# A two-block transformer in float32 on one core: five reorderings on TensorE around short waits

## What is computed

```python
def first_block(x, c, ...):
    h = _rmsnorm(x, norm_g[l]) * (1.0 + scale[:, None, :]) + shift[:, None, :]
    proj = h @ w_in[l]
    (q_a, k_a, v_a, z_a, q_b, k_b, v_b, z_b, f_logit, g_logit) = jnp.split(proj, split_points, axis=-1)
    y_a = _from_heads(_stick_breaking(q_a, k_a, v_a))
    y_a = (y_a * jax.nn.silu(z_a)) @ w_o_sb[l]
    log_f = jax.nn.log_sigmoid(f_logit + b_forget[l])
    cum_log_f = jnp.cumsum(log_f, axis=1).transpose(0, 2, 1)
    y_b = _from_heads(_forgetting_attention(q_b, k_b, v_b, cum_log_f))
    ...
    x = x + gate[:, None, :] * (merged @ w_out[l])
    return _rmsnorm(x, final_g)

def second_block(x, mem, ...):
    h = h + hybrid_mixer(rmsnorm(h, norm_mix_g[l]), ...)
    h = h + cross_attention(rmsnorm(h, norm_cross_g[l]), rmsnorm(mem, norm_mem_g[l]), ...)
    h = h + conv_ffn(rmsnorm(h, norm_ffn_g[l]), ...)
    return rmsnorm(h, norm_final_g[l])
```

## Time and profile before

| | us |
|---|---|
| median of 3 runs | 1424.27 (1421.89 to 1424.64) |
| the profiled execution's own time | 1422.05 |
| its span in the trace | 1420.2 |
| TensorE busy with matmuls | 1303.5 (92%), 6164 records |
| VectorE / GpSimd / ScalarE busy | 794.9 / 751.6 / 575.3 |
| mean granted TensorE clock | 0.969 of full |

### The profile page before, as it was taken

How to read it: one execution, slowest core, us unless ns; L and a number is a source line. 1 busy time by engine, 2 the same in 40 slices (tenths; PEclk the granted TensorE clock), 3 DMA queues, 4 the chain that set the end, 5 groups by cost and what they waited for, 6 DMA issues and landing times.

```text
span 1420.2 us, 16997 instructions
## 1 busy us (share of the span) xinstructions
PE 1303.5 (92%) x6164; PEld 1062.7 (75%) x6164; DVE 794.9 (56%) x1339; ACT 575.3 (41%) x926; POOL 751.6 (53%) x866
## 2 busy tenths in 40 slices
PE   3689999988999899899998789999999999999996
PEld 2567878867888777687776688787778888888874
DVE  5746767513333346687688554775537724651644
ACT  3354556425555335422335454443434322331331
POOL 4353443332333375476443377832647966885771
PEclk9999999999999999999999799999999999999998
DMA  8531222322333552222222334321222332323221
GB/s 303 178 104 44 68 67 101 115 68 80 99 108 114 194 157 85 82 86 93 75 61 67 112 106 145 119 75 45 90 90 63 108 111 90 104 92 102 89 75 59
DMA packets 41699, 142.80 MB, mean 101 GB/s; under 512 B 4624, under 2 KB 5008, under 8 KB 40464
## 3 DMA queue, kind: packets, MB, share of 16 engines
q1 hardware_dynamic: 41616, 141.71, 30.8%
HBM read 131.21 MB, written 8.39 MB: 98 GB/s over the span
## 4 chain that ended last, share of the span: by engine, by line
PE 78%; DVE 12%; ACT 5%; issue 2%; DMA 1%; POOL 1%; SPq 0%; DVEq 0%; ACTq 0%; POOLq 0%
PE ps L135 77%; DVE tm L145 3%; DVE ma L148 1%; ACT wh L142 1%; ACT tm L142 1%; PE ps L139 1%; ACT L142 1%; DVE tm L148 1%; DMA con_raw<-con 1%; DVE ac L148 1%; ACT hh L142 1%; DVE sql L145 0%; DVE x L148 0%; POOL ycl L145 0%; POOL wl L145 0%
## 5 line engine op out<-in xcount | busy, mean ns | idle before, releaser
L145 POOL TENSOR_TENSOR wl<-raw,wh 128x256 fp32r<-128x256 f32 x804 | 681.5, 879 | 595.2 <-ACT wh L142 595.2
L142 ACT ACTIVATE wh<-raw 128x1024 fp32r<-128x1024 f32 x201 | 212.6, 1058 | 486.5 <-PE ps L135 474.5
L135 PE MATMUL ps<-hh,wh 128*128 128x512 f32 x872 | 345.5, 396 | 2.8 <-DVE cb L145 1.6
L135 PE MATMUL ps<-hl,wh 128*128 128x512 f32 x872 | 341.0, 391 | 0.0
L135 PE MATMUL ps<-hh,wl 128*128 128x512 f32 x872 | 340.9, 391 | 0.0
L135 PEld LDWEIGHTS ps<-hh,wh 128*128 128x128 f32 x872 | 164.9, 189 | 39.1 <-DVE cb L145 2.4
L135 PEld LDWEIGHTS ps<-hh,wl 128*128 128x128 f32 x872 | 164.3, 188 | 34.9
L135 PEld LDWEIGHTS ps<-hl,wh 128*128 128x128 f32 x872 | 164.8, 189 | 33.5 <-issue 0.5
L148 DVE SCALAR_TENSOR_TENSOR tm<-cb,par_sb,tm 128x512 f32<-128x512 f32 x88 | 87.5, 994 | 50.8 <-ACT tm L142 47.4
L145 DVE TENSOR_TENSOR tm<-tm,tm 128x512 f32<-128x512 f32 (+3 forms) x106 | 91.1, 863 | 35.3 <-ACT tm L142 32.5
L142 ACT ACTIVATE tm<-tm 128x512 f32<-128x512 f32 (+3 forms) x109 | 54.5, 532 | 86.8 <-DVE tm L148 81.2
(11 more groups left out here) (316 smaller groups left out, 2405.4 us busy)
## 6 DMA issues: line engine op xcount, KB each, us to landing
raw<-units SPq DMA_DIRECT2D x217, 512.0 KB, 3.5
kept<-ge SPq DMA_DIRECT2D x16, 256.0 KB, 2.0
tm<-kept SPq DMA_DIRECT2D x16, 256.0 KB, 3.8
tm<-gate_w SPq DMA_DIRECT2D x12, 256.0 KB, 4.1
x<-xin SPq DMA_DIRECT2D x2, 1024.0 KB, 6.6
x<-xin SPq DMA_DIRECT2D x1, 2048.0 KB, 12.2
out<-x SPq DMA_DIRECT2D x8, 256.0 KB, 2.1
kv<-kvt SPq DMA_DIRECT2D x1, 1536.0 KB, 8.5
```

What stands on the lines that cost most here:

```text
L135: return self.none if self.e is None else self.e.matmul(out, lhs, rhs, start=start, stop=stop, skip_group_check=skip)
L142: return self.none if self.e is None else self.e.activation(out, in_, func, **kw)
L145: return self.none if self.e is None else self.e.tensor_tensor(out, a, b, op)
```

## The change

Five things are done; every instruction is still there, on the same engine.

1. The first q, k, z take banks 0, 1 and 7 (`qkz_bank`), and stand in the order q, k, z in the units and on TensorE and ScalarE.
2. In head 0, the q unit of `beside_a` goes ahead of `cum_a(0)` on TensorE, and its high and low parts go ahead of `cum_a(0)` on ScalarE and VectorE.
3. `forget` is cut in three and called from `vproj("b")`: the logits' unit ahead of value unit 0, the turns ahead of unit 2, the sums ahead of unit 3.
4. In `out_proj` the unit that follows is done in three pieces: chunks 0 to 3 ahead of `add(6)`, 4 to 6 between `add(6)` and `add(7)`, 7 behind `add(7)`.
5. `spread("m2")` goes behind the next unit, u1, and on VectorE the copy of its result and `scale_x` go behind the first steps on u1 and u5.

```diff
-    u += [("aq", 0), ("az", 0), ("ak", 0)]
+    u += [("aq", 0), ("ak", 0), ("az", 0)]
...
+        def pieces(gen, name, b):
+
+            def piece(x):
+                chunks(name, b, ((0, 1, 2, 3), (4, 5, 6), (7,))[x], x == 0, x == 2, lambda k: HH[:, k, :],
+                       lambda k: HL[:, k, :], lambda k: (s_hh, gen, k), lambda k: (s_hl, gen, k))
+            return piece
...
-        def vproj(br, nm, gen):
+        def vproj(br, nm, gen, between=None):
             for u in range(4):
+                if between:
+                    between(u)
...
-        def forget():
-            hhalf("1", ("f", 0), 0, 1)
-            hhalf("1", ("f", 0), 1, 1)
-            pe.wait_ge(s_fd, "log")
+        def forget(u):
+
+            if u == 0:
+                hhalf("1", ("f", 0), 0, 1)
+                hhalf("1", ("f", 0), 1, 1)
+            if u == 2:
+                pe.wait_ge(s_fd, "log")
...
+            if u == 3:
+                pe.wait_ge(s_fd, "turned")
...
         qkz("a", 0, "q", 1)
+        qkz("a", 0, "k", 0)
+        qkz("a", 0, "k", 1)
         qkz("a", 0, "z", 0)
         qkz("a", 0, "z", 1)
-        qkz("a", 0, "k", 0)
-        qkz("a", 0, "k", 1)
...
             br, c = z_step(h)
+            if h == 0:
+                beside_a(br, c, h // 2, h % 2 == 0)
             cum_a(h)
-            beside_a(br, c, h // 2, h % 2 == 0)
+            if h:
+                beside_a(br, c, h // 2, h % 2 == 0)
...
-        forget()
-
-
-        vproj("b", "bv", "1")
+
+
+        vproj("b", "bv", "1", forget)
...
+            following(0)
             add(6)
-            following()
+            following(1)
             add(7)
+            following(2)
...
-        hhalf("m", ("u", 0), 1, 0)
         hproj("m", ("u", 4), 1)
         spread("m", 7, TM[4])
         bank[7] = (s_root, ("m", "out"))
-        spread("m2", 6, TM[3])
-        bank[6] = (s_root, ("m2", "out"))
...
             if j:
                 hproj("m", ("u", j), b0)
             bank[b0] = (s_ux, (j, 0))
+            if j == 1:
+                spread("m2", 6, TM[3])
+                bank[6] = (s_root, ("m2", "out"))
...
+    def qkz_bank(br, c, what):
+        return {"q": 0, "k": 1, "z": 7}[what] if (br, c) == ("a", 0) else {"q": 0, "k": 0, "z": 1}[what]
...
         qk_high("a", 0, "q")
         root("mem", ncol("mem", 2))
+        qk_high("a", 0, "k")
         z_gate("a", 0)
-        qk_high("a", 0, "k")
...
-        spread_out("m2", 6, YF[:, 0, :])
...
-            if j == 0:
+            if j == 1:
+                spread_out("m2", 6, YF[:, 0, :])
                 scale_x(range(KC))
```

More of the change, by code:

```diff
@@ L563, in qkz @@
         def qkz(br, c, what, part):
-            b = {"q": 0, "k": 0, "z": 1}[what]
+            b = qkz_bank(br, c, what)
             hhalf("1", (br + what, c), part, b)
@@ L638, in pv_a @@
             bank[b] = (s_gy, ("a", h))
-        def forget():
-            hhalf("1", ("f", 0), 0, 1)
-            hhalf("1", ("f", 0), 1, 1)
-            pe.wait_ge(s_fd, "log")
[L644 to L653, removed]
+        def forget(u):
[4 more added lines that the diff above has]
+                pe.wait_ge(s_fd, "log")
+                for n in range(4):
+                    last = pe.turn(PS[1][:, 8 * n:8 * n + 8], TM[1][0:8, 128 * n:128 * n + 128], con_raw[0:8, 16:24])
+                last.then_inc(*s_fp.up("turn"))
+            if u == 3:
+                pe.wait_ge(s_fd, "turned")
+                for n in range(4):
+                    for b in range(n + 1):
+                        last = pe.mm(PS[1][0:8, 128 * n:128 * n + 128], TM[0][:, 8 * b:8 * b + 8],
+                                     con_f("triu" if b == n else "one"), b == 0, b == n)
+                last.then_inc(*s_fp.up("sum"))
+                bank[1] = (s_fd, ("f",))
         vproj("a", "av", "1")
@@ L790, in out_proj @@
                 take(6)
+            following(0)
             add(6)
-            following()
+            following(1)
             add(7)
+            following(2)
             bank[7] = (s_root, (gen, "mult"))
         out_proj("wo", "m", (0, 1, 2), lambda k: mg((VBh, MG2h), k), lambda k: mg((VBl, MG2l), k),
-                 lambda k: (s_mh, k), lambda k: (s_ml, k), lambda: hhalf("m", ("u", 0), 0, 0), both=True)
+                 lambda k: (s_mh, k), lambda k: (s_ml, k), pieces("m", ("u", 0), 0), both=True)
         bank[6] = (s_root, ("m2", "mult"))
-        hhalf("m", ("u", 0), 1, 0)
         hproj("m", ("u", 4), 1)
@@ L1013, in tensor_program @@
                 sub_out(3)
-        out_proj("wo2", "c", (2, 3, 4, 5), *yd, lambda: hhalf("c", ("cq", 0), 0, 0), lead=3, end=(3,))
-        hhalf("c", ("cq", 0), 1, 0)
+        out_proj("wo2", "c", (2, 3, 4, 5), *yd, pieces("c", ("cq", 0), 0), lead=3, end=(3,))
         bank[0] = (s_cqx, (0,))
@@ L1086, in tensor_program @@
                 pv_c(h)
-        out_proj("co", "f", (0, 1, 2), *o, lambda: hhalf("f", ("up", 0), 0, 0), lead=2, end=(6, 7))
+        out_proj("co", "f", (0, 1, 2), *o, pieces("f", ("up", 0), 0), lead=2, end=(6, 7))
         def up(f, b):
@@ L1107, in down @@
                 sums(("o", 7), 7, "o1024", 1, s_sqhd, s_sqld, False, True)
-        hhalf("f", ("up", 0), 1, 0)
         bank[0] = (s_cb, (0,))
@@ L1251, in qk_high @@
             d, s = {"q": (Qh, s_qh), "k": (Kh, s_kh)}[what]
-            act.fn(d[p][:, :], PS[0][:, :], ACT.Copy).then_inc(*s.up(br, c))
+            act.fn(d[p][:, :], PS[qkz_bank(br, c, what)][:, :], ACT.Copy).then_inc(*s.up(br, c))
         def z_gate(br, c):
@@ L1260, in z_gate @@
                 act.wait_ge(s_yl, *before_z(br, c))
-            act.fn(SZ[c % 2][:, :], PS[1][:, :], ACT.Silu).then_inc(*s_sz.up(br, c))
+            act.fn(SZ[c % 2][:, :], PS[qkz_bank(br, c, "z")][:, :], ACT.Silu).then_inc(*s_sz.up(br, c))
         def gate(n):
@@ L1307, in scalar_program @@
             br, c = z_step(h)
+            if h == 0:
+                qk_high(br, c, "q")
             cum_a(h)
-            qk_high(br, c, "qk"[h % 2])
+            if h:
+                qk_high(br, c, "qk"[h % 2])
             if h < 7:
@@ L1781, in qk_low @@
                 dve.wait_ge(s_qh, br, c)
-                split_low(Ql[p][:, :], PS[0][:, :], Qh[p][:, :], (br, c), s_ql)
+                split_low(Ql[p][:, :], PS[qkz_bank(br, c, "q")][:, :], Qh[p][:, :], (br, c), s_ql)
             if step == 3:
                 dve.wait_ge(s_kh, br, c)
-                split_low(Kl[p][:, :], PS[0][:, :], Kh[p][:, :], (br, c), s_kl)
+                split_low(Kl[p][:, :], PS[qkz_bank(br, c, "k")][:, :], Kh[p][:, :], (br, c), s_kl)
         def gate_y(br, h, dh, dl):
@@ L1847, in vector_program @@
             br, c = z_step(h)
+            if h == 0:
+                qk_low(br, c, 1)
             cum_a(h)
-            qk_low(br, c, 3 if h % 2 else 1)
+            if h:
+                qk_low(br, c, 3 if h % 2 else 1)
             if h < 7:
@@ L2395, in pool_program @@
             low(UNITS[j])
-        for name in UNITS[N_ADA:PLACE["ak", 0] + 1]:
+        for name in UNITS[N_ADA:PLACE["az", 0] + 1]:
             refill(name)
         pool.zero(f32(FT[:, :])).then_inc(*s_fz.up(0))
-        for name in UNITS[PLACE["ak", 0] + 1:PLACE["oa", 0]]:
+        for name in UNITS[PLACE["az", 0] + 1:PLACE["oa", 0]]:
             refill(name)
```

## The result

The changed kernel takes 1401.44 us in the median of 4 runs (1400.03 to 1410.39), the kernel before 1424.45 in 4 runs beside it; the ratio is 0.985, with a 95% interval of 0.9804 to 0.9896. In a later group of runs it was 1401.76 against 1423.6, ratio 0.983 (0.9813 to 0.9848). One of that group's six runs was in a slow state of the chip, with 1882.14 us at a granted clock of 0.655; it is in the median and not in the ratio. The forecast was 1402.2. The profiled execution took 1402.02, with a span of 1400.2 and a mean granted clock of 0.975 (before: 1420.2 and 0.969). So the spans differ by 20.0, the medians by 23.0. TensorE's idle times over 0.15 us add up to 91.1 us, where they were 107.8.

What follows compares the result with a forecast made beforehand. TensorE was taken to bound the kernel (78% of the span), its waits and half-clock time being the gain. Terms -5.2 - 8.5 - 5.5 - 2.9 = -22.1 took 1424.27 to 1402.2 us; range 1396.5 to 1410.0.

Steps and rivals of the forecast that it cites:

- q, k, z and q ahead of cum_a(0): Head 0: TensorE's waits of 1.92 and 4.74 us go, but VectorE's chain limits the gain to 5.2 us.
- forget in three: Forget: value units fill the 6.26 us wait for log f, and turns and sums run at full clock; 8.5 us gained.
- norm m with m2: Norm m: unit pieces fill waits for squares' parts and m2's spread no longer waits 1.73 us; u5 starts 5.5 us earlier.
- norms c and f: At norms c and f, pieces of the following unit remove TensorE's waits; 1.45 us each, together 2.9.
- cum_a(0) starts at 103.1 at full clock: Head 0: with the q unit filling the wait for `sph`, cum_a(0) starts at 103.1 us, not 104.35 at half clock.
- it waits there longer: TensorE waits over the earlier 1.58 us for k's low part at 138.57, leaving only VectorE's 5.2 us gain.
- short waits keep the clock down: Rival, chance 0.12: short waits in norm m and cum_a(0) bring back 1.2 GHz; gain only 15.4 us, 1408.9.
- the cover holds with 1.8 us to spare: Behind norm m, VectorE's idle 5.54 us before `rtl` absorbs the moved `scale_x`, leaving 1.8 us spare.
- those named as right: Confirming signs: named waits gone, earlier starts, some 16 us less TensorE idle time, slowed `sph` and `spl`, longer qk_a(2) wait.
- the longer wait at qk_a(2): Sign in head 0: TensorE waits over 1.58 us at qk_a(2).
- the three named as wrong: Refuting signs: wait for `rtl` at second block's first q, over 2 us for values' low parts, 0.50 clock around u0.

Runs made afterwards that it cites:

- wh behind ewl: Changed kernel, but in head 0 ScalarE makes the next `wh` only once VectorE is through with `ewl`, moving GpSimd's pass beside PSUM-reading instructions; 1401.58 us.
- late wh: Changed kernel, but in head 0 ScalarE makes the next `wh` behind the exps of cum_a(0), not ahead of the moved q's high part; 1402.74 us.
- order q, z, k: Changed kernel with only the first units' order and banks put back (banks 0 and 1); the q unit stays ahead of cum_a(0); 1403.92 us.
- norm m filled: Changed kernel; at norm m, half of u4 stands between m2's first sums and the last sums, and m's spread in mid u1; 1400.89 us.

## Why the prediction held, step by step

| step | forecast | measured |
|---|---|---|
| q, k, z and q ahead of cum_a(0) | -5.2 | -6.2 |
| forget in three | -8.5 | -8.0 |
| norm m with m2 | -5.5 | -4.4 |
| norms c and f | -2.9 | -3.0 |
| sum | -22.1 | -21.6 |

The measured column follows the same instructions through both profiles. The rest to the spans' 20.0 is the later beginning (0.55) and stretches at half clock at instructions that no edit touches: 0.4 lost at those behind 312 and 520, one at 687 gone (1.5), 0.5 gained between 751 and 850, one at 957 new (1.6), one at 1349 longer (1.0). Head 0 came out 1.0 above its forecast, forget 0.5 and norm m 1.1 below; that the sum is off by 0.5 only is in part luck.

- **Head 0: right on VectorE, wrong on the clock.** VectorE's last `spl` was forecast to end at 109.3 and head 1 to start at 112.8; with the later beginning taken out they are at 109.0 and 112.6. "cum_a(0) starts at 103.1 at full clock" held until 110 only, and "it waits there longer" at 138.57 failed: half clock from 111 to 118 slowed TensorE to VectorE's pace, so that it met no wait. The run with wh behind ewl has the wait, 1.88, and no such stretch. Of the rival "short waits keep the clock down" the half-clock stretch came, but its cause isn't borne out: it came also where the waits ahead were 0.15 and 0.23 (late wh) or 0.11 (order q, z, k), and with 0.15 and 0.23 it stayed away (wh behind ewl). What VectorE decides is 4.75 at qk_a(2) and 4.6 at qk_a(4), 0.5 short of the forecast; the rest to 6.2 is the shorter half clock behind qk_a(4), which I had not counted, and which is luck.
- **Forget: right, 0.5 short.** I priced turns and sums at half of their time at half clock, 2.2. They take 0.4 and 2.3. The cover for log f, for the copy behind the turns and for `ft` held: neither turns nor sums wait, and the wait at qk_b(0) stayed 1.50.
- **Norm m: the term was mis-sized.** TensorE reached u5 5.0 earlier (counted from the norm's beginning), 0.5 short: half clock from 568 to 572 cost 0.3 up to u4, and m2's spread takes 0.9 of TensorE's time, not 0.5. Then "the cover holds with 1.8 us to spare" was wrong. I had added up VectorE's instructions at their durations of before. `scale_x` took 8.2 from its start to the next instruction's, not 7.2, and the 14 taps from 623.81 on 16.2, not 14.6. VectorE was some 3 us later than the sum and cost TensorE 0.9 at the wait, 0.6 after the next unit. The traces tie this to GpSimd's passes: from 575 to 662 of the changed kernel an instruction of `scale_x` or the taps takes 0.75 us where GpSimd does nothing beside it, in 4 cases, and 1.14 in the mean where a pass lies all over it, in 29; in the kernel before it is 0.75 in 7 and 1.13 in 16. GpSimd is busy for 6.1 us of `scale_x`, before 4.6, and for 16.1 us of the 14 taps, before 11.6. No run moved the passes there by themselves.
- **Norms c and f: right.** 1.5 each; undone they cost 1.5 each.
- **The level.** By the profiled executions the change is worth 20.0, not 22.1. The forecast stood on the median of before, and the medians are 23.0 apart (21.8 in the later group); so part of its closeness (0.8) is owed to which executions were profiled.
- **The signs.** Of those named as right, all came but the longer wait at qk_a(2): TensorE's idle time is 16.7 less, and of the slices of 1 us 79 lie below a clock of 0.97, before 99. Of the three named as wrong two came: the wait at the first q of the second block (1.16) and clock rows of 0.50 around u0 (568 to 572, though 4 us where the kernel before had 8). Both lie in norm m, whose term fell short.

## What to carry to other kernels

Where an in-order engine that bounds the kernel waits, a piece of later work of about that length can be put ahead of the wait, if each follower on the other engines keeps its order; pieces that belong to different places added up here. Work moved on a second engine has to be priced at durations beside its new neighbours, with the idle time ahead of the next instruction that the bounding engine needs as the budget; and a pass moved out of one chain's way can bring the next pass into the next chain's. And a gain of 1 or 2 us in one place isn't read from one median: follow the same instruction through both traces.

## What the runs showed of the chip

- TensorE's granted clock falls to 1.2 GHz in stretches in which it has no idle time in the records, at the small matmuls of the scores (64 rows) and behind waits. Shortening the waits ahead of one (0.55, 0.75 and 0.64, down to 0.15 and 0.23) didn't remove it; bringing the next head's work forward by 2 us, with the same two short waits, moved it from 111 to 133. What decides its start stays open.
- The stretches and their places were the same in the two profiled executions of the changed kernel, and its runs still differ by 12.0 us (1398.4 to 1410.4), at granted clocks from 0.977 to 0.968.
- A stretch at half clock and a wait can stand for one another: at the turns of branch b the changed kernel had half clock from 312 to 319 and a wait of 2.96, the kernel with norm m filled half clock from 310 to 321 and 1.67.
- A GpSimd pass and VectorE instructions from SBUF to SBUF slow one another: 0.69 became 1.10 us and 0.75 became 1.14, and a piece of the pass 0.71 became 0.97. Beside VectorE instructions that read PSUM neither was slowed (0.68, 0.69 and 0.71).
